# Feed-forward jobs run in pairs, product by product, with in-place quads kept twice

## The chip, the cores and the metric

One NeuronCore of one Trainium2 chip runs the whole kernel. The metric is the device time of one execution in microseconds. The kernel before took 2522.27 us, the median of three runs (2521.65 to 2526.93).

## What is computed

The reference is a trunk of two residual layers on a sequence of 1024 tokens and a width of 1024, all in float32. Layer 0 has a state-space and a gated-recurrence mixer, layer 1 has windowed attention. Behind each mixer comes the part that the change is about:

```
hn = rms_norm(h, mlp_norm[i])                                    # 1024 x 1024
h  = h + square(relu(hn @ w_mlp_in[i])) @ w_mlp_out[i]           # 1024 x 4096, 4096 x 1024
```

An embedding gate follows each of them, and a last RMS norm. The jobs into which it is cut may run in any order that keeps their inputs ahead of them.

## The kernel before, in words

**A float32 product in three passes.** Each operand is split into a high part (rounded to the matmul's type) and a low part (the rest), and each tile product is made of high by high, high by low and low by high. Weights are split while they stream in: ScalarE rounds (`high`, all its instructions stand in the trace at line L1348), VectorE or GpSimd subtracts (`weight_low`, L2323, and `low`, L578).

**Jobs and products.** Both matrix products of the feed-forward block use a 2 by 2 block scheme with seven block products instead of eight. A job is one pair of 128-wide output blocks by both halves of the tokens, with one weight slab of 1 MB, and has seven products, 0 to 6. A product is 12 matmuls of 512 columns (4 contraction tiles by 3 passes), at L1099. There are 32 jobs: 16 up (into the 4096-wide middle), then 16 down in four chunks of four jobs; a chunk uses the middle blocks of four up jobs. So one feed-forward block has 224 products, and the kernel has two such blocks. TensorE takes the jobs one after the other, product by product.

**Weights of a job.** The slab lands in `SRAW` (two buffers in turns, a third for the last job). GpSimd makes four sums of quarters (`sum_`, L573) in `SA` and `SB`, one buffer each, and the low parts of products 0, 3 and 6; VectorE makes the low parts of 1, 2, 4 and 5. High and low parts lie in a ring of five. ScalarE rounds four products ahead, VectorE subtracts three ahead.

**PSUM.** A job has three banks, and two jobs in turns have six. Products 0 and 3 add up in the first, 1, 4 and 6 in the second, 2 and 5 in the third. Between two products of a bank its partial value is read out: product 3 waits for the copy of product 0, product 4 for the eviction of product 1, and so on.

**Behind an up job.** ScalarE copies product 0 to `P1` (`first_product`); VectorE adds bank values to make `U2`, `V5` and the four quads `Q` (`evict_up`, L2332 to L2345), multiplies them by the reciprocal norm (`scaled`, L2350 to L2352), ScalarE does relu and square (`squared`) into four of the seven blocks of `MT`, VectorE makes the other three (`mid_sums`, L2357 to L2362), and SP stores the seven blocks of the job to DRAM in one transfer (L345).

**Refill.** The seven operands `OP` are used by every job of a chunk. When product s of the last job of a chunk is done, SP loads the new block s (L351, 1 MB), ScalarE rounds it in two halves (`cast`), and VectorE subtracts in two halves (`refill`, L2401). Product s of the next job needs it seven products later. There are four refills in a block: ahead of down jobs 16, 20, 24 and 28. In a down job VectorE adds each bank to the residual (`evict_down`, L2374 to L2387).

**Start.** The first job's operands are made from the residual as the projection ahead of it comes out (`x_operands`); operands 4, 5 and 6 are made after that (`x_late`, `cast_late` on ScalarE, `late_difference`, `late_last`, `block_low` on VectorE, L2305 to L2316), and the sums of squares and the reciprocal root follow.

**Order.** Each engine has its order written out by hand: a loop over t, the product that TensorE has reached, with what is due at each t. An engine does its list in order, so a wait holds all that stands behind it.

## Time and profile before

| what | value |
|---|---|
| median of 3 runs | 2522.27 us |
| profiled execution, its own time | 2522.98 us |
| its span, first to last instruction | 2521.2 us |
| TensorE busy | 2321.1 us, 92% |
| VectorE, GpSimd, ScalarE busy | 1611.7, 1066.9 and 980.9 us |
| mean granted TensorE clock | 0.966 of full speed |
| first feed-forward block, its products | 543 to 1218 us of the span |
| second one | 1700 to 2375 us |

The profile is one execution. Busy time is a share of the whole span. A matmul's own duration overlaps the next one's, so the pace is read from how many run in a stretch, and a stretch has to be asked for by its ends. The granted clock is 1.00 at 2.4 GHz and 0.50 at 1.2 GHz; a mean between them mixes both.

### The profile page before, as it was taken

What the parts mean: (1) busy time and instruction counts of PE and PEld (TensorE: products, weight loads), DVE (VectorE), ACT (ScalarE), POOL (GpSimd) and SP (SyncE); (2) the same over time, 40 slices, a digit from 0 to 9 for tenths busy, and PEclk for the clock granted to TensorE, in tenths of its full rate; (3) what the DMA queues carried; (4) which work ended last, traced back from release to release, by engine and by line L of the source; (5) the groups of instructions that cost most, each with busy time, mean ns of one, the idle gap of its engine ahead of it and who ended that gap; (6) DMA issues with size and microseconds to landing.
All of it is one profiled execution on the core that took longest, in us unless ns stands there. A gap on an engine that the chain in (4) does not pass through costs nothing.

```text
span 2521.2 us, 31322 instructions
## 1 busy us (share of the span) xinstructions
PE 2321.1 (92%) x12286; PEld 1858.2 (74%) x12286; DVE 1611.7 (64%) x1959; ACT 980.9 (39%) x1526; POOL 1066.9 (42%) x684
## 2 busy tenths in 40 slices
PE   8998967997999989999998999987999989999997
PEld 6887856776888877777786776665888867877786
DVE  6867279558676766648627355567767676467725
ACT  3120255443444534433312245644444454334315
POOL 4433112234555545545332343634555545455421
PEclk9998978999999999999999999998999999999998
DMA  7372331212344634433113111111444464324111
GB/s 209 106 120 74 112 110 61 92 44 106 138 154 167 224 110 167 167 117 100 51 50 100 40 28 51 59 42 34 168 146 161 153 225 167 118 100 164 54 50 67
DMA packets 216867, 277.85 MB, mean 110 GB/s; under 512 B 32548, under 2 KB 171016, under 8 KB 212616
## 3 DMA queue, kind: packets, MB, share of 16 engines
q1 hardware_dynamic: 203176, 257.13, 30.5%
q10 hardware_dynamic: 13552, 18.81, 3.0%
q8 instruction: 94, 1.54, 0.3%
q14 instruction: 45, 0.37, 0.0%
HBM read 190.53 MB, written 84.21 MB: 109 GB/s over the span
## 4 chain that ended last, share of the span: by engine, by line
PE 71%; DVE 20%; ACT 4%; issue 3%; POOL 1%; ACTq 1%; DMA 0%; DVEq 0%; SPq 0%; POOLq 0%
PE ps L1099 39%; PE ps L727 15%; DVE op L2401 6%; PE ps L1265 3%; PE ps L878 2%; PE ps L1297 2%; DVE st_lo L2323 1%; PE ps L1225 1%; DVE hg_queries_keys L2166 1%; DVE residual L2387 1%; PE ps L1238 1%; PE ps L1249 1%; PE ps L899 1%; PE ps L914 1%; PE ps L794 1%
## 5 line engine op out<-in xcount | busy, mean ns | idle before, releaser
L1099 PE MATMUL ps<-op,st_hi 128*128 128x512 f32 x3584 | 1134.5, 398 | 93.1 <-DVE op L2401 39.3
L1099 PEld LDWEIGHTS ps<-op,st_hi 128*128 128x128 f32 x3584 | 683.1, 192 | 261.8 <-issue 100.3
L1099 PE MATMUL ps<-op,st_lo 128*128 128x512 f32 x1792 | 709.1, 396 | 0.0
L578 POOL TENSOR_TENSOR st_lo<-st_raw,st_hi 128x512 fp32r<-128x512 f32 x192 | 323.9, 1687 | 631.2 <-ACT st_hi L1348 631.2
L1099 PEld LDWEIGHTS ps<-op,st_lo 128*128 128x128 f32 x1792 | 343.5, 192 | 73.3
L1348 ACT ACTIVATE st_hi<-st_sum 128x512 fp32r<-128x512 f32 x256 | 160.3, 630 | 436.6 <-POOL st_sum L573 232.1
L557 POOL CAST w_hi<-w_raw 128x1024 fp32r<-128x1024 f32 x66 | 74.1, 1123 | 482.2 <-issue 249.3
L2387 DVE TENSOR_TENSOR residual<-residual,ps 128x512 f32<-128x512 f32 x192 | 131.3, 684 | 192.6 <-PE ps L1099 191.2
L1348 ACT ACTIVATE st_hi<-st_raw 128x512 fp32r<-128x512 f32 x192 | 120.6, 628 | 262.4 <-PE ps L1099 262.4
L573 POOL TENSOR_TENSOR st_sum<-st_raw 128x512 f32<-128x512 f32 x128 | 180.9, 1413 | 57.9 <-DVE st_lo L2323 57.9
L2323 DVE TENSOR_TENSOR st_lo<-st_sum,st_hi 128x512 fp32r<-128x512 f32 x256 | 193.9, 758 | 0.4
L727 PE MATMUL ps<-x_hi,w_hi 128*128 128x512 f32 x544 | 170.3, 394 | 7.5 <-DVE x_lo L2407 3.7
L727 PE MATMUL ps<-x_lo,w_hi 128*128 128x512 f32 x544 | 167.7, 390 | 0.0
L727 PE MATMUL ps<-x_hi,w_lo 128*128 128x512 f32 x544 | 167.6, 389 | 0.0
L2401 DVE TENSOR_TENSOR op<-op_raw,op 128x1024 fp32r<-128x1024 f32 x112 | 167.1, 1531 | 0.0
L559 POOL TENSOR_TENSOR w_lo<-w_raw,w_hi 128x1024 fp32r<-128x1024 f32 x66 | 161.6, 2448 | 5.3
L1348 ACT ACTIVATE op<-op_raw 128x1024 fp32r<-128x1024 f32 (+2 forms) x150 | 141.1, 988 | 32.3 <-DVE op_raw L2316 21.6
L727 PEld LDWEIGHTS ps<-x_hi,w_hi 128*128 128x128 f32 x544 | 101.0, 188 | 33.4 <-issue 6.6
L727 PEld LDWEIGHTS ps<-x_hi,w_lo 128*128 128x128 f32 x544 | 102.1, 188 | 21.5
L727 PEld LDWEIGHTS ps<-x_lo,w_hi 128*128 128x128 f32 x544 | 102.1, 188 | 21.4
L573 POOL TENSOR_TENSOR st_sum<-st_sum,st_raw 128x512 f32<-128x512 f32 x64 | 98.0, 1531 | 5.0
L573 POOL TENSOR_TENSOR st_sum<-st_raw,st_sum 128x512 f32<-128x512 f32 x64 | 94.3, 1474 | 0.0
(343 smaller groups left out, 3407.4 us busy)
## 6 DMA issues: line engine op xcount, KB each, us to landing
mid_dram<-mid_sums SPq DMA_DIRECT2D x32, 1792.0 KB, 5.7
op_raw<-mid_dram SPq DMA_DIRECT2D x56, 1024.0 KB, 6.1
st_raw<-w_mlp_in_in SPq DMA_DIRECT2D x32, 1024.0 KB, 5.4
st_raw<-w_mlp_out_in SPq DMA_DIRECT2D x32, 1024.0 KB, 5.3
w_raw<-w_in_even_in SPq DMA_DIRECT2D x20, 512.0 KB, 4.5
residual_dram<-residual ACTq DMA_DIRECT2D x2, 4096.0 KB, 12.4
w_raw<-w_ple_gate_in SPq DMA_DIRECT2D x16, 512.0 KB, 4.1
residual<-residual_dram SPq DMA_DIRECT2D x3, 2048.0 KB, 8.6
```

What stands on the lines that cost most here:

```text
L557: pool.tensor_copy(WH[:, b, :], RAW[:, b, :]).then_inc(S["w_hi_done"], 1)
L559: pool.tensor_tensor(WL[:, b, :], RAW[:, b, :], WH[:, b, :].bitcast(F32), ALU.subtract).then_inc(S["w_ready"], 1)
L573: pool.tensor_tensor(o[:, :, :], x, y, op).then_inc(S["st_sum"], 1)
L578: pool.tensor_tensor(SL[r][:, :, :], x, SH[r][:, :, :].bitcast(F32), sub).then_inc(S["st_lo_pool"], 1)
L727: ins = pe.matmul(acc[:, h, :], w[:, k, :], x[:, k0 + k, h * HALF:(h + 1) * HALF], start=(k == 0 and w is wh and x is xh), stop=(k == kts ...
L878: ins = pe.matmul(ACC[u % 2][:, h, :], w[:, k, :], x[:, k, h * HALF:(h + 1) * HALF], start=(k == 0 and w is wh and x is XAh), stop=(k == K ...
L1099: ins = pe.matmul(PS[:, o, :], w[:, j, :], OP[s][:, x, j, :], start=(s < 3 and j == 0 and w is SH[r] and x == 0), stop=(j == 3 and w is SL ...
L1265: ins = pe.matmul(PS[:, h, :], w[:, k, :], x[:, k, h * HALF:(h + 1) * HALF], start=(k == 0 and w is whs[s % 2] and x is XAh), stop=last)
L1348: return act.activation(o, i, f, **kw)
L2323: tt(SL[r][:, :, :], (SB if s in (1, 5) else SA)[:, :, :], SH[r][:, :, :].bitcast(F32), sub).then_inc(S["st_lo"], 1)
L2387: tt(h, h, PS[:, x, :], add).then_inc(S["st_ev"], 1)
L2401: tt(OP[s][:, 1, 2 * h:2 * h + 2, :], OPF[s][:, 1, 2 * h:2 * h + 2, :], OP[s][:, 0, 2 * h:2 * h + 2, :].bitcast(F32), sub)\
```

## The change

The two jobs of a pair are run product by product: 0 of the first, 0 of the second, 1 of the first, and so on, 14 products to a set. Only the last pair keeps the old order. Every engine's list is written for sets. The sum buffers `SA` and `SB`, and the quads `Q`, are there twice. An up job's partial values are built in its own quads (`P1`, `U2` and `V5` are gone); ScalarE copies product 0 and product 3 from PSUM; one VectorE operation takes the maximum with zero and multiplies by the reciprocal norm; ScalarE squares all four quads in place with one instruction; four differences follow, one of them in place, two in `MT` and one in `T4`, which there is once. The stores of a job are three: quads (1 MB), two sums (0.5 MB), last sum (0.25 MB), and the copy of a later job's product 0 waits for the first of these to land. A refill's halves are spread over 14 products, one per product. A first down product is copied by ScalarE. Half of the making of operand 6 goes from VectorE to GpSimd. The blocks' order in DRAM follows the stores.

```diff
+def product_at(n):
+
+    k, r = divmod(n, 2 * SLOTS)
+    b, s = divmod(r, SLOTS) if k == SETS - 1 else (r % 2, r // 2)
+    return 2 * k + b, s
...
+    SA, SB = ([at(f"st_sum{b}{x}", [P, 4, P], F32, MISC_AT + (4 + 4 * b + 2 * x) * K) for b in range(2)] for x in range(2))
+    Q = [at(f"quads{b}", [P, 4, HALF], F32, o) for b, o in enumerate((E1_AT, MISC_AT + 12 * K))]
+    MT = [at(f"mid_sums{b}", [P, 2, HALF], F32, E1_AT + (8 + 4 * b) * K) for b in range(2)]
+    T4 = at("mid_last_sum", [P, HALF], F32, E0_AT + 12 * K)
...
+                def store_set(g):
+                    sp.wait_ge(S["q_ready"], UP * i + g + 1)
+                    sp.dma_start(t_dram[i][g][:, 0:4, :], Q[g % 2][:, :, :]).then_inc(stored[g % 2], 16)
+
+                def store_sums(g):
+                    sp.wait_ge(S["mt_ready"], UP * i + g + 1)
+                    sp.dma_start(t_dram[i][g][:, 4:6, :], MT[g % 2][:, :, :]).then_inc(mt_stored[g % 2], 16)
+
+                def store_last(g):
+                    sp.wait_ge(S["t4_ready"], UP * i + g + 1)
+                    sp.dma_start(t_dram[i][g][:, 6, :], T4[:, :]).then_inc(S["t4_stored"], 16)
...
+                    if k >= SETS // 2 and k % 2 == 0 and r == 0 and k < SETS - 1:
+                        refill((k - SETS // 2) // 2, 6)
+                    if k >= SETS // 2 - 1 and k % 2 and r and r % 2 == 0 and k < SETS - 1:
+                        refill((k - SETS // 2 + 1) // 2, r // 2 - 1)
+                    if 1 <= k <= SETS // 2:
+                        if r == 3:
+                            store_set(g - 2)
+                        if r == 4:
+                            store_set(g - 1)
+                            store_sums(g - 2)
+                            store_last(g - 2)
+                        if r == 5:
+                            store_sums(g - 1)
+                        if r == 6:
+                            store_last(g - 1)
+                    if r in (9, 10) and k < SETS - 1:
+                        b = r - 9
+                        sp.wait_ge(S["st_lo_pool"], low_pool(i, g + b, 6))
+                        raw(g + 2 + b)
+                sp.wait_ge(S["st_lo_pool"], low_pool(i, JOBS - 3, 6))
...
+                    pool.wait_ge(S["st_lo"], low_dve(i, g, 2))
+                    pool.tensor_tensor(sum_of(g, 4), quarter(g, 0, 0), quarter(g, 1, 0), sub).then_inc(S["st_sum"], 1)
+                    pool.tensor_tensor(sum_of(g, 5), quarter(g, 0, 1), sum_of(g, 1), sub).then_inc(S["st_sum"], 1)
...
+                def late_operand():
+                    pool.wait_ge(S["op_x_scaled"], X_SCALED * i + 10)
+                    pool.wait_ge(S["op_x_sum"], X_SUMS * i + 9)
+                    pool.wait_ge(S["op_ready"], READY * i + 12)
+                    pool.tensor_tensor(OPF[6][:, 1, :, :], OPF[6][:, 1, :, :], OP[1][:, 0, :, :].bitcast(F32), sub).then_inc(S["op_x_sum"], 1)
+
+                for k in range(SETS - 1):
+                    for g in (2 * k, 2 * k + 1):
+                        first_sum(g)
+                        low(g, 0)
+                        second_sum(g)
+                    for g in (2 * k, 2 * k + 1):
+                        low(g, 3)
+                    if k == 0:
+                        late_operand()
+                    for g in (2 * k, 2 * k + 1):
+                        last_sums(g)
+                    for g in (2 * k, 2 * k + 1):
+                        low(g, 6)
...
+                for n in range(PRODUCTS):
+                    g, s = product_at(n)
...
+                        x = sum_of(g, s)
                     fn(SH[n % RINGS][:, :, :], x, ACT.Copy).then_inc(S["st_hi"], 1)
 
-                def first_product(g):
-                    act.wait_ge(S["st_prod"], sb + SLOTS * g + 1)
-                    if g:
-                        act.wait_ge(S["st_ev"], ev(i, g - 1, 5))
-                    fn(P1[:, :], PS[:, BANKS[g % 2][0], :], ACT.Copy).then_inc(S["st_p1"], 1)
+                def copy(g, s):
+                    a_, b = BANKS[g % 2][0], g % 2
+                    act.wait_ge(S["st_prod"], made(i, g, s))
+                    if s == 3:
+                        fn(Q[b][:, 0, :], PS[:, a_, :], ACT.Copy).then_inc(S["st_p1"], 1)
+                    elif g < UP:
+                        if g >= 2:
+                            act.wait_ge(*set_stored(i, g - 2))
+                            act.wait_ge(S["t4_ready"], UP * i + g - 1)
+                        elif g == 1:
+                            act.wait_ge(S["ss_done"], norm + 1)
+                        fn(Q[b][:, 1, :], PS[:, a_, :], ACT.Copy).then_inc(S["st_p1"], 1)
+                    else:
+                        act.wait_ge(mt_stored[(g - UP) // 2], 16 * (UP // 2) * (i + 1))
...
-                    act.wait_ge(S["q_scaled"], n + 1)
-                    for h in range(2):
-                        fn(Q[:, 2 * h:2 * h + 2, :], Q[:, 2 * h:2 * h + 2, :], ACT.Relu).then_inc(S["q_relu"], 1)
...
+                cast_late(i, 5, 9, 9)
+                high(9)
...
+                    dve.wait_ge(S["op_x_sum"], X_SUMS * i + 10)
...
+                    _, b_, c_ = BANKS[g % 2]
+                    q = Q[g % 2]
+                    dve.wait_ge(S["st_prod"], made(i, g, s))
+                    if s < 3:
+                        dve.wait_ge(S["st_p1"], copied(i, g, 0))
+                        tt(q[:, 4 - s, :], q[:, 1, :], PS[:, (b_, c_)[s - 1], :], add).then_inc(S["st_ev"], 1)
+                    elif s == 6:
+                        tt(q[:, 1, :], q[:, 1, :], PS[:, b_, :], add).then_inc(S["st_ev"], 1)
                     else:
-                        tt(Q[:, 1, :], P1[:, :], PS[:, b_, :], add).then_inc(S["st_ev"], 1)
+                        dve.wait_ge(S["st_ev"], ev(i, g, 6 - s))
+                        tt(q[:, s - 2, :], q[:, s - 2, :], PS[:, (b_, c_)[s - 4], :], add).then_inc(S["st_ev"], 1)
 
                 def scaled(g):
-                    dve.wait_ge(S["st_ev"], ev(i, g, 5))
+                    q = Q[g % 2]
+                    dve.wait_ge(S["st_ev"], ev(i, g, 6))
+                    dve.wait_ge(S["st_p1"], copied(i, g, 3))
                     dve.wait_ge(S["rstd_done"], norm + 1)
-                    tt(Q[:, 0, :], PS[:, BANKS[g % 2][0], :], RSTD[:, lefts], ALU.mult).then_inc(S["st_c11"], 1)
-                    tt(Q[:, 2:4, :], Q[:, 2:4, :], RSTD[:, rights].unsqueeze(1).to_broadcast([P, 2, HALF]), ALU.mult)
-                    tt(Q[:, 1, :], Q[:, 1, :], RSTD[:, lefts], ALU.mult).then_inc(S["q_scaled"], 1)
-
-                def mid_sums(g):
-                    n = UP * i + g
-                    dve.wait_ge(S["q_squared"], 2 * n + 2)
-                    tt(MT[:, 4, :], MT[:, 5, :], MT[:, 2, :], sub)
-                    tt(MT[:, 2, :], MT[:, 2, :], MT[:, 0, :], sub).then_inc(S["mt_sum"], 1)
-                    dve.wait_ge(S["mt_sum"], 2 * n + 1)
-                    tt(MT[:, 1, :], MT[:, 5, :], MT[:, 2, :], sub).then_inc(S["mt_sum"], 1)
-                    dve.wait_ge(S["mt_sum"], 2 * n + 2)
-                    tt(MT[:, 6, :], MT[:, 3, :], MT[:, 1, :], sub).then_inc(S["mt_ready"], 1)
+                    for h, t in ((0, lefts), (2, rights)):
+                        ins = dve.scalar_tensor_tensor(q[:, h:h + 2, :], q[:, h:h + 2, :], 0.0, RSTD[:, t].unsqueeze(1).to_broadcast([P, 2, HALF]),
+                                                       ALU.max, ALU.mult)
+                    ins.then_inc(S["q_scaled"], 1)
...
+                def first_mid_sums(g):
+                    q, mt, n = Q[g % 2], MT[g % 2], UP // 2 * i + g // 2
+                    dve.wait_ge(S["q_squared"], UP * i + g + 1)
+                    if n:
+                        dve.wait_ge(mt_stored[g % 2], 16 * n)
+                    tt(mt[:, 0, :], q[:, 3, :], q[:, 0, :], sub)
+                    tt(q[:, 3, :], q[:, 2, :], q[:, 3, :], sub).then_inc(S["q_ready"], 1)
+
+                def second_mid_sum(g):
+                    q, mt = Q[g % 2], MT[g % 2]
+                    dve.wait_ge(S["q_ready"], UP * i + g + 1)
+                    tt(mt[:, 1, :], q[:, 2, :], mt[:, 0, :], sub).then_inc(S["mt_ready"], 1)
+
+                def last_mid_sum(g):
+                    dve.wait_ge(S["mt_ready"], UP * i + g + 1)
+                    if i or g:
+                        dve.wait_ge(S["t4_stored"], 16 * (UP * i + g))
+                    tt(T4[:, :], Q[g % 2][:, 1, :], MT[g % 2][:, 1, :], sub).then_inc(S["t4_ready"], 1)
...
-                            return
+                        if c == 1:
+                            dve.wait_ge(S["st_p1"], copied(i, UP + q, 0))
...
+                block_low(4, 17)
+                for s in (1, 2):
+                    evict_up(0, s)
+                weight_low(8)
+                for s in (1, 2):
+                    evict_up(1, s)
+                weight_low(9)
+                block_low(5, 18)
+                weight_low(10)
                 late_last()
+                weight_low(11)
+                evict_up(0, 4)
+                evict_up(1, 4)
                 block_low(6, 19)
...
+                for p in range(2):
+                    reciprocal(p)
+                evict_up(0, 5)
+                evict_up(1, 5)
...
+                    if k < SETS // 2:
+                        if r in (6, 7):
+                            for s in (1, 2):
+                                evict_up(g + r - 6, s)
+                        if r >= 9:
+                            evict_up(g + (r - 9) % 2, 4 + (r - 9) // 2)
+                    if 1 <= k <= SETS // 2 and r == 0:
+                        evict_up(g - 1, 6)
+                    if t > UP * SLOTS and product_at(t - 1) not in COPIES:
+                        evict_down(*product_at(t - 1))
                     if t + 3 < PRODUCTS:
...
+                    if k < SETS // 2 and r == 13:
+                        scaled(g)
+                    if 1 <= k <= SETS // 2:
+                        if r == 0:
+                            scaled(g - 1)
+                        if r == 2:
+                            first_mid_sums(g - 2)
+                        if r == 3:
+                            first_mid_sums(g - 1)
+                            second_mid_sum(g - 2)
+                            last_mid_sum(g - 2)
+                        if r == 4:
+                            second_mid_sum(g - 1)
+                        if r == 5:
+                            last_mid_sum(g - 1)
+                    kj, rj = divmod(t - 6, 2 * SLOTS)
+                    if kj >= SETS // 2 - 1 and kj % 2 and kj < SETS - 1:
+                        refill((kj - SETS // 2 + 1) // 2, rj // 2, rj % 2)
...
+                    if k == SETS - 1 and r < SLOTS and 2 <= r <= 5:
+                        add_squares(after, r - 2)
+                    if k == SETS - 1 and r in (SLOTS + 3, SLOTS + 5):
+                        add_squares(after, 4 + (r - SLOTS - 3) // 2)
```

## Rows read from the trace of the kernel before

**Rows 1.** The page: share of each engine in the chain that ended last.

```profile
PE 71%; DVE 20%; ACT 4%; issue 3%; POOL 1%; ACTq 1%; DMA 0%; DVEq 0%; SPq 0%; POOLq 0%
```

**Rows 2.** Windows, product matmuls alone: stretch, length, busy (count), clock, DMA share, GB/s.

```profile
543.00:624.60 81.60, 60.99 (x240) 0.90 0.18 62
624.60:861.60 237.00, 236.95 (x1045) 1.00 0.42 156
861.60:899.30 37.70, 29.40 (x121) 0.92 0.80 295
899.30:958.80 59.50, 59.50 (x253) 0.96 0.34 122
958.80:988.00 29.20, 23.68 (x97) 1.00 0.57 204
988.00:1044.30 56.30, 56.30 (x241) 0.97 0.29 100
...
1129.80:1161.00 31.20, 25.20 (x97) 0.89 0.54 191
```

**Rows 3.** Timeline of TensorE, 550 to 585 us, where it had been idle.

```profile
557.96 1.19 PE L1099 MATMUL ps<-op,st_hi 128*128 128x512 f32 x2 [5.94 <-ACT p L1348]
...
569.70 0.70 PE L1099 MATMUL ps<-op,st_hi 128*128 128x512 f32 x2 [2.24 <-DVE op L2305]
...
581.21 1.19 PE L1099 MATMUL ps<-op,st_hi 128*128 128x512 f32 x2 [8.51 <-DVE quads L2341]
```

**Rows 4.** Chain, 955 to 990 us: start, us, what.

```profile
960.08 2.27 DVE op L2401 x2
...
964.07 3.36 DVE op L2401 x2
967.43 0.60 DVE residual L2387
```

**Rows 5.** Groups by form, 955 to 990 us: count, busy us, mean ns, idle before.

```profile
L2401 DVE TENSOR_TENSOR op<-op_raw,op 128x1024 fp32r<-128x1024 f32 x14 | 21.8, 1597 | 0.0
...
L578 POOL TENSOR_TENSOR st_lo<-st_raw,st_hi 128x512 fp32r<-128x512 f32 x5 | 8.7, 1743 | 12.2 <-ACT st_hi L1348 12.2
...
L2387 DVE TENSOR_TENSOR residual<-residual,ps 128x512 f32<-128x512 f32 x9 | 6.1, 678 | 4.1 <-PE ps L1099 4.1
...
L573 POOL TENSOR_TENSOR st_sum<-st_raw 128x512 f32<-128x512 f32 x2 | 4.3, 2170 | 3.1 <-DVE st_lo L2323 3.1
```

**Rows 6.** Groups by form, 700 to 738 us, an up stretch.

```profile
L578 POOL TENSOR_TENSOR st_lo<-st_raw,st_hi 128x512 fp32r<-128x512 f32 x6 | 10.4, 1732 | 17.5 <-ACT st_hi L1348 17.5
...
L573 POOL TENSOR_TENSOR st_sum<-st_raw 128x512 f32<-128x512 f32 x4 | 5.2, 1294 | 0.0
...
L1348 ACT ACTIVATE quads<-quads 128x1024 f32<-128x1024 f32 x4 | 4.0, 1042 | 0.0
```

**Rows 7.** Line L2407: count, duration ns min/median/max, first and last start.

```profile
L2407 DVE SCALAR_TENSOR_TENSOR x_lo<-residual,vectors,x_hi x16: 1278/1286/3411, 1213.6 to 2389.3; 128x1024 fp32r<-128x1024 f32 x16
```

**Rows 8.** Timeline of VectorE at the start, operand 6.

```profile
569.48 3.37 DVE L2315 TENSOR_TENSOR op_raw<-op_raw,op 128x2048 f32<-128x2048 f32 x1
```

**Rows 9.** Timeline of GpSimd at the start.

```profile
570.66 3.31 POOL L578 TENSOR_TENSOR st_lo<-st_raw,st_hi 128x512 fp32r<-128x512 f32 x1
```

**Rows 10.** DMA issues: count, KB each, median us to landing.

```profile
mid_dram<-mid_sums SPq DMA_DIRECT2D x32, 1792.0 KB, 5.7
op_raw<-mid_dram SPq DMA_DIRECT2D x56, 1024.0 KB, 6.1
st_raw<-w_mlp_in_in SPq DMA_DIRECT2D x32, 1024.0 KB, 5.4
...
fqig_dram<-stage SPq DMA_DIRECT2D x11, 512.0 KB, 3.1
```

**Rows 11.** Windows, all engines: stretch, length, busy (count), clock, DMA share, GB/s.

```profile
862.00:878.00 16.00, 16.00 (x73) 13.23 (x72) 13.45 (x15) 12.20 (x16) 10.18 (x7) 1.00 1.04 376
988.00:996.00 8.00, 8.00 (x28) 6.45 (x29) 3.51 (x6) 1.27 (x2) 2.91 (x3) 0.79 0.00 0
```

391 lines of the change are left out of this document (185 added, 206 removed).

## The prediction

> **What bounds the kernel now.** The page gives 71% of the last-ending chain to TensorE and 20% to VectorE [rows 1]. That is the mean over very different stretches, so the windows over the product matmuls come next [rows 2]. In a long stretch of up jobs 1045 matmuls take 237.0 us, 0.2268 us each, so a product (12) takes 2.72 us at full clock: the floor. The 2688 matmuls of a block need 609.6 us and take 675.4 us (543.0 to 1218.4). The excess of 66 us is what a new order can win, 132 us in two blocks. Count times 0.2268 taken from each stretch's length puts it in place [rows 2]:
>
> - start (240 matmuls): 81.6 - 54.4 = 27.2 us
> - refill for job 16 (121): 37.7 - 27.4 = 10.3 us
> - refills for 20 and 24 (97 each; the second's row, 1044 to 1073 us, repeats the first's): 29.2 - 22.0 = 7.2 us each
> - refill for 28 (97): 31.2 - 22.0 = 9.2 us
> - stretches right behind refills: 59.5 - 57.4 = 2.1, then 56.3 - 54.7 = 1.6, twice: 5.3 us.
>
> The last item is the clock: in the 8 us behind a refill TensorE is never idle yet runs 28 matmuls instead of 35, at a granted 0.79, a mix of the levels 1.2 and 2.4 GHz, after a stretch with gaps [rows 11].
>
> In a refill the chain is almost all VectorE: two subtractions of 128x1024 take 2.27 us undisturbed and 3.36 us when a GpSimd instruction falls among them; an eviction takes 0.60 [rows 4]. Seven products bring 14 such halves. They have the VectorE full, and product s+7 waits for them.
>
> At the start three gaps stand out [rows 3]: 5.94 us for the copy of product 0 (ScalarE was still making operands), 2.24 us for a late operand, and 8.51 us at product 6, whose operand ends a chain through both engines.
>
> **The change, part by part.** I write r for the product's place in a set of 14; one step is 2.72 us.
>
> *Refills of jobs 20, 24, 28.* Now 14 products (38.1 us) stand between the release of an operand and its need. VectorE owes 14 halves at 1.14 (16.0), 14 evictions at 0.60 (8.4) and 8 low parts at 0.60 (4.8): 29.2 us. GpSimd disturbs: 14 halves in the old refill were busy 21.8 us instead of 16.0 [rows 5], 5.8 us for the 8 or 9 GpSimd instructions beside them, 0.7 each; there will be 14, 9.8 us. Sum 39.0 us against 38.1: level, with seven products' slack for the halves and about two for a low part queued behind one. But in such stretches GpSimd's sums stretch from 1.29 to 2.17 us [rows 5, 6], and a pair's slabs are freed only at r = 9 and 10, so its chain gets tight. Of 7.2 + 7.2 + 9.2 + 3.2 us (the clock items behind them) = 26.8 I leave 5.5: gain 21.3 (bounds 11 and 26.8).
>
> *Refill of job 16.* It meets the end of the last up pair: 10 evictions (6.0), 14 halves (16.0), 8 low parts (4.8), four fused operations, eight differences (4.8), three down evictions (1.8). The fused operation (maximum, then multiply, 128x1024) isn't in the trace; its nearest row is another two-input operation of that class, 1.28 us at the least and 3.41 at the most [rows 7], and a plain one takes 1.14 [rows 4]. I take 1.2, as it stands beside similar work: 4.8. Sum 38.2, with GpSimd 48 us against 38.1: VectorE falls 10 us behind. The deadline it breaks is new: the copy of job 16's product 0 waits until the sums of job 14 are stored, for they share memory, and ScalarE and product 3 wait with it. VectorE's list reaches that sum some 41 us into the window, the store lands about 4 us later, and product 3 is due at 38: a gap of 7 to 8 us. I leave 9.5 of 10.3 + 2.1: gain 3 (bounds -6 and 12.4). DMA is near its limit here too: 376 GB/s at a full share [rows 11].
>
> *Start.* Product 3 comes at place 6, product 4 at 8 and product 6 at 12, so the 5.94 and 2.24 us gaps close, and the chain for operand 6 has 14 us more. Against that, half of operand 6 goes to GpSimd. VectorE's 3.37 us [rows 8] become four times 1.29 = 5.2 us [rows 6], or four times 3.31 = 13 beside a busy VectorE [rows 9]; I take 8, between them, since both engines are half busy there. Four sums and so the weights of product 4 queue behind it: gaps of 2 us at place 8 and 2 us at place 12. Then the reciprocal root is ready only when both jobs are over, `scaled` of both holds VectorE's low parts: 2.5 us. With the first wait for the last operand (3.2), the four norm matmuls (1.5) and a cold clock for a short time (2) I leave 13 of 27.2: gain 14 (bounds 7 and 22). The Trainium skill (GPSIMD Engine Reference, section 3.1) gives 4.5 us for such a float32 operation of 2048 elements, 1.96 times VectorE's. By that the gap at place 8 would vanish and the block be 2 us shorter; the row with both engines busy says the opposite.
>
> *Up jobs.* Now no gap at all [rows 2]. VectorE keeps five evictions and four differences; three multiplications (0.60, 1.14, 0.60) become two of about 1.2; ScalarE drops two relus of 1.04 us [rows 6], gains a copy of about 0.6. All of it lies under TensorE: nothing gained. The new wait is the release of the quads. Second job of a pair: `scaled` done at about 5.7 us of the set, square 7.9, differences 10.7, store sent, landed by 10.7 + 5.4 to 6.1 [rows 10] = 16 to 17, copied 17.5; product 3 of the next job wants it at 19.1. A slack of 1.6 us: I charge 1 us per block (0 to 15). ScalarE waits there with the next `high` behind it, which has two products of slack.
>
> *Nothing elsewhere:* the tail keeps its order, the slabs' size and the matmuls are the same. SP issues 3 stores instead of one and is idle most of the time.
>
> **Sum.** 21.3 + 3 + 14 - 1 = 37.3 us a block; the second block shows the same gaps, so 75 us in two. The profiled execution took 2523.0 us (span 2521.2 plus 1.8), the median 2522.3, so they are alike. Forecast 2522.3 - 75 = 2447 us. Bounds: 26.8 + 12.4 + 22 = 61 a block, 2400 us; 11 - 6 + 7 - 15 = -3, 2528 us, all ends bad at once.
>
> **Rivals.**
> *A. VectorE and GpSimd stay the bound.* If a disturbance costs 1.1 us (3.36 - 2.27) [rows 4] and not 0.7, each set with a refill owes 44.6 us against 38.1, its slack is used up, and the start gains only 7: 11 + 0 + 7 - 1 = 17 a block, 2488 us. For it: the row. Against: not every instruction of GpSimd collided.
> *B. Everything is covered.* 55 us or more a block, 2410 us. Against: job 16's refill.
> *C. The release of the quads is late in every up pair.* The slack of 1.6 us is small. If landing takes 10 us, the store is in at 20.7 and copied at 21.3, 2.2 us late; seven sets in two blocks make 31 us: 2478 us. In its favour, the three stores of a job and those of the next run at once. By the Trainium skill (DMA: Bandwidth & Descriptors, anatomy of one DMA) a transfer from GpSimd costs a fixed 2 us plus its bytes at 436 GB/s: three stores pay the fixed part three times, and 1 MB would land in 4.4 us, before the deadline. The trace agrees, with 5.7 us for 1.75 MB and 3.1 us for 0.5 MB. Those two rows are what speaks against C [rows 10].
> *D. Slower: the slab hand-over.* Both slabs of a pair are used to nearly the end of the set. The first is free at r = 8.9, lands at 10.9 (5.4 us) [rows 10], then GpSimd does sum, low part, sum, sum, low part: 1.29, 1.73, 1.29, 1.29, 1.73 = 7.3 us [rows 6], to r = 13.6. It is due at r = 15, a slack of 3.9 us. It decides from the point where landing plus those five take over 3.9 us more. At 2.17 us for each sum it's 2.6 more, inside. Only if landing took 10 us as well would each of 30 hand-overs lose 3.3 us, 99 us in all: 2447 + 99 = 2546 us.
> *E. No difference:* the gaps move and keep their size; 2522.
>
> **Chances.** Forecast 0.60, A 0.16, B 0.12, C 0.07, D 0.04, E 0.01. The range leaves out D and about half of B and takes in A and C: 2412 to 2490. A measurement of this kernel can tell about 0.2% (5 us) from no change. Faster 0.95, same 0.01, slower 0.04.
>
> **What would show it.** The stretch from the first product to job 2's end should take 14 us less; gaps before 20, 24 and 28 nearly gone, VectorE still about 95% busy there; one gap of 7 to 8 us in job 16 at product 3, released by a ScalarE copy that waited for a store; the clock at 1.00 behind refills; the up sets without gaps. Wrong would be: gaps in each up set before product 3 of the second job (C), gaps before products 0 and 1 of each pair (D), or GpSimd's busy time up by over a tenth (A).

## The result, and the profile after

The changed kernel takes 2493.76 us, the median of four runs (2487.47 to 2495.61). The kernel before took 2521.96 us beside it (2521.4 to 2526.93). The ratio is 0.988, its 95% interval 0.9861 to 0.9898: faster, by 28 us, which is 1.2% and clear of the scatter. The forecast was 2447 us and 75 us faster, in a range of 2412 to 2490. So the sign was right and the size was wrong: 28 of 75 us came, and the time lies above the range.

The profiled execution took 2494.89 us (span 2493.2). Its page, busy time of four engines and the chain's shares:

```profile
PE 2314.5 (93%) x12286; PEld 1860.1 (75%) x12286; DVE 1642.3 (66%) x1917; ACT 939.2 (38%) x1470; POOL 1092.2 (44%) x686
...
PE 64%; DVE 18%; issue 5%; ACT 5%; DMA 4%; POOL 2%; ACTq 1%; SPq 0%; DVEq 0%; POOLq 0%
```

DMA was 0% of the chain [rows 1] and is 4% now, half of it for slabs of the down weights; VectorE went from 20% to 18%. The shares don't say which wait is new; the windows and the timelines do. The windows over the product matmuls (now at line L1202) of the first block show where, with the columns of [rows 2]:

```profile
543.00:640.00 97.00, 83.55 (x333) 0.91 0.24 82
640.00:820.00 180.00, 177.04 (x776) 1.00 0.41 149
820.00:860.10 40.10, 35.03 (x155) 0.97 0.60 209
860.10:923.00 62.90, 53.40 (x214) 0.91 0.53 189
923.00:985.00 62.00, 62.00 (x275) 1.00 0.50 166
985.00:1132.00 147.00, 147.00 (x650) 1.00 0.47 158
1132.00:1204.50 72.50, 66.89 (x286) 0.98 0.15 44
```

With the floor of 0.2268 us a matmul the excess of each part is its length less its count times 0.2268:

| part of the block | before | forecast | after | how the last is worked out |
|---|---|---|---|---|
| start | 27.2 | 13 | 21.5 | 97.0 - 333 x 0.2268 |
| up jobs | 0 | 1 | 4.0 | 180.0 - 776 x 0.2268 |
| refill for job 16, with the end of the last up pair | 12.4 | 9.5 | 19.3 | 103.0 - 369 x 0.2268 |
| refills for 20, 24 and 28 | 26.8 | 5.5 | 6.8 | 281.5 - 1211 x 0.2268 |

The four add up to 51.6 us where 66.4 were before, 14.8 us a block. Measured from the first product matmul to the last, the first block went from 677.6 to 662.1 us and the second from 683.6 to 667.4, 31.7 us in all. Between the blocks 2.9 us were lost, the start and the tail of the span changed by under 1 us: 28.0 us of the span.

So the largest term held within 1.3 us, and three did not hold. A place is a product's position in the block, counted from 0; a set of a pair has 14 places. These are the stalls of TensorE in the first block (timeline, what it waited for in brackets; smaller ones of 0.2 to 1.3 us are left out):

```profile
569.18 1.19 PE L1202 MATMUL ps<-op,st_hi 128*128 128x512 f32 x2 [4.22 <-ACT quads L1451]
601.90 1.22 PE L1202 MATMUL ps<-op,st_hi 128*128 128x512 f32 x2 [2.72 <-DVE st_lo L2447]
616.31 1.19 PE L1202 MATMUL ps<-op,st_hi 128*128 128x512 f32 x2 [4.57 <-ACT quads L1451]
...
860.15 1.19 PE L1202 MATMUL ps<-op,st_hi 128*128 128x512 f32 x2 [5.13 <-ACT quads L1451]
...
907.78 1.19 PE L1202 MATMUL ps<-op,st_hi 128*128 128x512 f32 x2 [7.58 <-issue]
1135.22 0.73 PE L1202 MATMUL ps<-op,st_hi 128*128 128x512 f32 x2 [2.14 <-DVE st_lo L2447]
1141.00 1.22 PE L1202 MATMUL ps<-op,st_hi 128*128 128x512 f32 x2 [2.76 <-DVE st_lo L2447]
```

**The refills of 20, 24 and 28.** No stall stands ahead of jobs 20 and 24, and the clock is 1.00 behind them, where the stretch of before had 0.79 [rows 11]. A half still takes 1616 ns on the mean, much as in [rows 5], but now 38.1 us lie between release and need. By form, VectorE from 923 to 985 us, around the refill for 20:

```profile
L2518 DVE TENSOR_TENSOR op<-op_raw,op 128x1024 fp32r<-128x1024 f32 x12 | 19.4, 1616 | 4.2 <-ACT op L1451 4.2
L2510 DVE TENSOR_TENSOR residual<-residual,ps 128x512 f32<-128x512 f32 x18 | 12.3, 683 | 16.4 <-PE ps L1202 16.4
L2447 DVE TENSOR_TENSOR st_lo<-st_sum,st_hi 128x512 fp32r<-128x512 f32 x12 | 11.0, 923 | 1.5 <-ACT st_hi L1451 1.5
```

VectorE was nearly never free in the refill of before (4.1 us, [rows 5]); here it is idle 22 us of 62. This window holds 12 of the 14 halves and nine products ahead of them; while the halves run, VectorE is busy 32.0 us of 38:

```profile
947.00:985.00 38.00, 32.00 (x33) 1.00 0.58 195
```

That is 84%, where the forecast had about 95%. The stalls of 2.14 and 2.76 us in the refill for 28 come where the last chunk adds the stored first sums to the residual.

**The first stall of the start, 4.22 us.** Product 3 of job 1 needs the copy of job 1's product 0. On ScalarE that copy stands behind the rounding for product 8, which waits for a sum of GpSimd. Three timelines, ScalarE's, GpSimd's and VectorE's:

```profile
567.92 0.63 ACT L1451 ACTIVATE st_hi<-st_sum 128x512 fp32r<-128x512 f32 x1 [7.02 <-POOL st_sum L664]
568.46 0.58 ACT L1451 ACTIVATE quads<-ps 128x512 f32<-128x512 f32 x1
```

```profile
559.95 4.61 POOL L676 TENSOR_TENSOR op_raw<-op_raw,op 128x2048 f32<-128x2048 f32 x1
564.51 3.32 POOL L664 TENSOR_TENSOR st_sum<-st_raw 128x512 f32<-128x512 f32 x1
```

```profile
561.00 5.70 DVE L2430 TENSOR_TENSOR op<-op_raw,op 128x2048 fp32r<-128x2048 f32 x1 [3.57 <-ACT op L1451]
```

The operand's half that the change gave to GpSimd took 4.61 us, where I had taken 8. That agrees with the Trainium skill (GPSIMD Engine Reference, section 3.1: 4.5 us). The sum behind it took 3.32 us, as [rows 9], and VectorE's operation beside both took 5.70 us, where one of that size had taken 3.37 [rows 8]. The three rows read as waits for each other's end: VectorE's started at 561.0, GpSimd's ended at 564.5, and VectorE's ended 2.1 us behind that, about what it takes alone (2.28 at 572.5); the sum started at 564.5 and ended 1.1 us behind VectorE's, about as long as an undisturbed one (1.29). The stall is at place 7 and about as long as the two of 2 us that I had for places 8 and 12; GpSimd's late operand delays it, as I had it, but through the copy and not through the weights of product 4.

**The other two stalls of the start.** They stand in the chain behind the root. ScalarE's timeline, ahead of it:

```profile
595.14 0.63 ACT L1451 ACTIVATE st_hi<-st_sum 128x512 fp32r<-128x512 f32 x1 [3.57 <-POOL st_sum L660]
595.79 1.28 ACT L1451 ACT_TABLE_LOAD   x1
597.09 1.06 ACT L1451 ACTIVATE rstd<-rstd 128x1024 f32<-128x1024 f32 x1
```

VectorE, which had ended its reciprocals at 592.5, stood 4.39 us until the root, then did two fused operations, and the low part for product 17 behind them came late (2.72 us). Squares, differences and last sum follow, and the copy of job 2's product 0 waits for the last sum (4.57 us). The expectations below speak of this stall as the one in front of job 2's first product; what waits is product 3, whose bank that copy empties. The 2.72 us stand at place 17; where an expectation says product 15, this one is meant.

**The refill of job 16.** The gap at its product 3 is 7.58 us, as forecast (7 to 8 us). TensorE's row names no releaser (`issue`), so ScalarE's timeline has to say what the copy stood for: first a sum of GpSimd, then the store.

```profile
903.03 0.63 ACT L1451 ACTIVATE st_hi<-st_sum 128x512 fp32r<-128x512 f32 x1 [5.88 <-POOL st_sum L664]
907.09 0.60 ACT L1451 ACTIVATE p_sum<-ps 128x512 f32<-128x512 f32 x1 [3.42 <-DMA mid_dram<-mid_sums]
```

The other one, 5.13 us ahead of product 3 of job 15, was not in my sum. VectorE waits with job 13's last sum until job 12's has been stored, since there is one buffer of them, and the copy of job 15's product 0 waits for it (VectorE, then ScalarE):

```profile
858.60 0.69 DVE L2489 TENSOR_TENSOR mid_last_sum<-quads,mid_sums 128x512 f32<-128x512 f32 x1 [4.65 <-DMA mid_dram<-mid_last_sum]
```

```profile
859.41 0.60 ACT L1451 ACTIVATE quads<-ps 128x512 f32<-128x512 f32 x1 [5.51 <-DVE mid_last_sum L2489]
```

The tile's own view says how such a store lands, and who waits for the sums in the whole run:

```profile
  ACT quads L1451: 62.3, 28
...
DMA to landing us min/median/max: 2.0/2.4/7.9
```

The late one is a transfer of 256 KB, issued at 850.58 us in the middle of three refill loads of 1 MB (841.5, 846.9, 852.6) and four other stores of 0.5 and 1 MB. In the up sets the same sum is the last thing that the copy waits for, 28 times: that is where the stalls of 0.2 to 1.3 us come from.

The medians from issue to landing, against [rows 10]:

```profile
op_raw<-mid_dram SPq DMA_DIRECT2D x56, 1024.0 KB, 5.2
...
mid_dram<-quads SPq DMA_DIRECT2D x32, 1024.0 KB, 3.9
...
mid_dram<-mid_sums SPq DMA_DIRECT2D x32, 512.0 KB, 3.5
```

### The profile page after: what moved, and what is told of

Read it like the earlier page. It is cut to its first block, busy times and chain, and to the rows that moved or that the text cites. A ratio compares the mean times of both kernels' runs of the same rounds, so it can differ in the third digit from the quotient of the medians.

```text
span 2493.2 us, 31423 instructions
## 1 busy us (share of the span) xinstructions
PE 2314.5 (93%) x12286; PEld 1860.1 (75%) x12286; DVE 1642.3 (66%) x1917; ACT 939.2 (38%) x1470; POOL 1092.2 (44%) x686
## 4 chain that ended last, share of the span: by engine, by line
PE 64%; DVE 18%; issue 5%; ACT 5%; DMA 4%; POOL 2%; ACTq 1%; SPq 0%; DVEq 0%; POOLq 0%
PE ps L1202 32%; PE ps L831 15%; PE ps L1368 3%; PE ps L982 2%; DMA st_raw<-w_mlp_out_in 2%; PE ps L1400 2%; DVE st_lo L2447 2%; DVE mid_sums L2483 2%; DVE mid_last_sum L2489 1%; ACT quads L1451 1%; PE ps L1328 1%; POOL st_lo L670 1%; DVE quads L2478 1%; DVE stage L1953 1%; DVE hg_queries_keys L2291 1%
## 5 line engine op out<-in xcount | busy, mean ns | idle before, releaser
L1202 PE MATMUL ps<-op,st_hi 128*128 128x512 f32 x3584 | 1128.7, 397 | 74.3 <-ACT quads L1451 31.7
L1202 PEld LDWEIGHTS ps<-op,st_hi 128*128 128x128 f32 x3584 | 682.5, 191 | 233.4 <-issue 61.7
L1202 PE MATMUL ps<-op,st_lo 128*128 128x512 f32 x1792 | 706.7, 394 | 0.0
L670 POOL TENSOR_TENSOR st_lo<-st_raw,st_hi 128x512 fp32r<-128x512 f32 x192 | 306.0, 1596 | 525.6 <-ACT st_hi L1451 524.8
L1202 PEld LDWEIGHTS ps<-op,st_lo 128*128 128x128 f32 x1792 | 342.2, 191 | 73.1
L2447 DVE TENSOR_TENSOR st_lo<-st_sum,st_hi 128x512 fp32r<-128x512 f32 x256 | 230.7, 910 | 10.9 <-ACT st_hi L1451 9.5
L2518 DVE TENSOR_TENSOR op<-op_raw,op 128x1024 fp32r<-128x1024 f32 x112 | 175.6, 1568 | 39.4 <-ACT op L1451 39.4
L1451 ACT ACTIVATE op<-op_raw 128x1024 fp32r<-128x1024 f32 (+2 forms) x150 | 147.0, 990 | 8.3 <-DVE op_raw L2439 5.8
L654 POOL TENSOR_TENSOR st_sum<-st_raw 128x512 f32<-128x512 f32 x64 | 86.6, 1352 | 107.2 <-DMA st_raw<-w_mlp_out_in 64.4
L831 PEld LDWEIGHTS ps<-x_hi,w_lo 128*128 128x128 f32 x544 | 102.1, 188 | 21.5
L2460 DVE TENSOR_TENSOR quads<-quads,ps 128x512 f32<-128x512 f32 x64 | 43.7, 685 | 112.4 <-PE ps L1202 112.4
L664 POOL TENSOR_TENSOR st_sum<-st_raw 128x512 f32<-128x512 f32 x64 | 113.2, 1768 | 6.5 <-DVE st_lo L2447 6.5
```

The source lines that it names most:

```text
L654: pool.tensor_tensor(sum_of(g, 2), quarter(g, 1, 0), quarter(g, 1, 1), add).then_inc(S["st_sum"], 1)
L664: pool.tensor_tensor(sum_of(g, 4), quarter(g, 0, 0), quarter(g, 1, 0), sub).then_inc(S["st_sum"], 1)
L670: pool.tensor_tensor(SL[r][:, :, :], x, SH[r][:, :, :].bitcast(F32), sub).then_inc(S["st_lo_pool"], 1)
L831: ins = pe.matmul(acc[:, h, :], w[:, k, :], x[:, k0 + k, h * HALF:(h + 1) * HALF], start=(k == 0 and w is wh and x is xh), stop=(k == kts ...
L1202: ins = pe.matmul(PS[:, o, :], w[:, j, :], OP[s][:, x, j, :], start=(s < 3 and j == 0 and w is SH[r] and x == 0), stop=(j == 3 and w is SL ...
L1451: return act.activation(o, i, f, **kw)
```

## The experiments

Each is the changed kernel with the edit shown or named; runs 12 to 14 start from the kernel of run 11. The first eight are one run each, beside the kernel before on the same chip (2527.87 us for the first four, 2527.17 for the next four). Since single runs scatter by some microseconds, I also give the length of the two feed-forward blocks in the profile, first product matmul to last. All are collected at the end of this section. They scatter too. In the six kernels that leave the start as it is (changed, 1, 2, 5, 6, 7), product 3 of job 2 comes 72.5 to 74.4 us after the first product in the first block and 78.6 to 80.5 in the second. In the six that change nothing between there and product 3 of job 16 (changed, 3, 4, 7, 8, 9), this stretch takes 288.2 to 291.5 us. So a block that differs by under some 4 us in one profile shows little by itself.

**1. The first down products of jobs 16 and 17 stay in PSUM (z_psum).** They no longer wait for the memory of the stored sums, and are moved there later, at r = 11 and 12.

```
 copy(g, s), g = 16, 17:
-    act.wait_ge(mt_stored[...]); act.wait_ge(S["t4_ready"], ...)
-    fn(Z1[g - UP][:, :], PS[:, a_, :], ACT.Copy)
+    fn(PS[:, 4 + g - UP, :], PS[:, a_, :], ACT.Copy)
```

> The changed kernel, but the first products of jobs 16 and 17 are copied at once into two PSUM banks that are free by then, and moved to SBUF five products later, so that job 16 waits for no store. Theory S (the 7.6 us gap of job 16 before its product 3 is the store of job 14's sums, which shares memory with the copy): that gap goes in both blocks, and what is left is below 3 us, about 2 x 8 us and some clock less, 2476 to 2480 us in all. Rival V (VectorE is simply too far behind there and the store wait only hides it): another gap of 5 us or more takes its place at product 3, 4 or 5 of job 16, released by VectorE, and the time stays within 5 us of 2494.

2487.66 us, ratio 0.984; blocks 2.1 and 4.9 us shorter. The stall at product 3 of job 16 fell from 7.58 to 4.06 us (in the second block from 7.60 to 4.09) and not to nothing: the wait for the store was 3.5 us of it. That lies between my two cases. What is left comes from GpSimd's timeline in this run, and ScalarE's:

```profile
891.73 8.28 POOL L670 TENSOR_TENSOR st_lo<-st_raw,st_hi 128x512 fp32r<-128x512 f32 x2 [7.78 <-ACT st_hi L1451]
```

and, with the window ended at 894 us, the first of the two alone:

```profile
891.73 6.61 POOL L670 TENSOR_TENSOR st_lo<-st_raw,st_hi 128x512 fp32r<-128x512 f32 x1 [7.78 <-ACT st_hi L1451]
```

```profile
901.77 0.63 ACT L1451 ACTIVATE st_hi<-st_sum 128x512 fp32r<-128x512 f32 x1 [5.89 <-POOL st_sum L664]
902.31 0.58 ACT L1451 ACTIVATE ps<-ps 128x512 f32<-128x512 f32 x1
```

One low part took 6.61 us and the next about 1.7, where the median of the run is 1.30 and the mean 1.6. VectorE ran from 891.3 to 897.1 without a break, each instruction with two inputs in SBUF and not slowed (0.68 and 1.21 us). The late low part ended 1.2 us after VectorE's first instruction with an input in PSUM had started (897.11). So it looks shut out and not slow; the rows show it, no run tests it. The copy stands in the queue behind a rounding that waits for the sum behind those low parts. The low part's excess of 5.3 us is more than the 4.06 us that are left.

**2. The refill for job 16 four products later (shift4).** Loads, roundings and subtractions are all moved by four places.

```
-                    kj, rj = divmod(t - 6, 2 * SLOTS)
+                    kj, rj = divmod(t - 6 - (4 if t < 14 * (SETS // 2 + 1) else 0), 2 * SLOTS)
```

> The changed kernel, with the refill for job 16 (loads, roundings, subtractions) four products later than now; the other refills stay. Theory D (the refill's loads and the seven stores of the last up pairs want the DMA at once, and the single buffer of the last sum, 7.9 us to landing there against a median of 2.4, holds VectorE and then ScalarE's copy): the 5.1 us gap before product 3 of job 15 goes, the last sum of job 12 lands in under 4 us, 2 x 5 us less. Rival V (VectorE's total work of 48 us in 38 is the cause): the same lateness comes four products later, the excess of this refill stays at 17 to 20 us a block and the time within 5 us of 2494.

2476.35 us, ratio 0.980; blocks 10.3 and 6.9 us shorter. The stall of 5.13 us is gone (0.27 left); the one at product 3 of job 16 grew from 7.58 to 9.27. The crowd of transfers was the cause of the first one: with the loads moved out of it, the store of the last sum lands in time (issued at 845.35, the next last sum runs at 848.65 without a wait). The roundings and subtractions moved too, but VectorE had stood 4.65 us for that store, so it was not short of time there. The gain of 17 us is more than the 10 I expected; some of it is scatter, since the two blocks differ by 3.4 us.

**3. On ScalarE the copy goes ahead of the rounding of product 8 (copy_first).**

```
-                high(8)
                 copy(1, 0)
+                high(8)
```

> The changed kernel, with one line of ScalarE's list moved: the copy of job 1's product 0 ahead of the rounding for product 8. Theory Q (the 4.2 us gap before product 7 is this copy standing behind a rounding that waits for GpSimd's sums, which wait for operand 6): the gap before product 7 is gone; the next one is product 8 for its low part, 1 to 2 us, so 2 to 3 us less a block, 2488 to 2490. Rival P (the start is bound by GpSimd's chain for operand 6 anyway): the gap moves to product 8 in full, 4 us, and the time is unchanged.

2494.11 us, ratio 0.987; blocks 0.2 and 1.5 us shorter, which is nothing. The stall of 4.22 us became 1.95, but two of GpSimd (0.61 and 2.47) came in before product 17. It was moved, not removed; the block is as long as before within the scatter.

**4. The late operand's half back on VectorE (operand6_vector).**

```
-                    if k == 0:
-                        late_operand()
 late_last():
+                    tt(OPF[6][:, 1, :, :], OPF[6][:, 1, :, :], OP[1][:, 0, :, :].bitcast(F32), sub)
```

> The changed kernel, with the first half of operand 6 put back on VectorE. Theory P (GpSimd's 4.6 us operation, with 5.7 us for the VectorE operation beside it, is what delays the start): the gap before product 7 shrinks from 4.2 to about 0 and nothing replaces it, up to 4 us less a block. Rival: VectorE has no room at the start either, its list gets 3.4 us longer, and a gap of 3 us or more appears at product 10 or 12, so the time is unchanged or higher.

2489.01 us, ratio 0.985; blocks 0.4 and 5.2 us shorter. The first stall became 0.37, and in its place stand 1.72, 2.45 and 1.15 us for low parts of GpSimd, then 2.31 and 4.43 as before. Product 3 of job 2 comes at 72.0 us and not at 72.5: again the start is not shorter in the first block.

**5. One and two together (shift4_z).**

> Both edits at job 16's refill: four products later, and the first products of jobs 16 and 17 copied into free PSUM banks. With the later refill alone the gap before product 3 of job 16 was 9.3 us, with the PSUM copies alone 4.1. Theory W (the copy has two waits in a row: the store, and behind it the rounding that stands ahead of it on ScalarE and waits for GpSimd's sums, which are held up by VectorE's unbroken run): with both edits the gap is 3 to 6 us and released by GpSimd's sums, 4 us less a block than the later refill alone, 2467 to 2470. Rival (the store alone was what counted, and the 4.1 us came from the crowd that the later refill has thinned out): gap under 1.5 us, 2460 or less.

2467.65 us, ratio 0.976; blocks 12.5 and 12.6 us shorter. The two gains add up in the blocks: 12.4 for the first, 11.8 for the second. The gap at product 3 of job 16 is 4.06 us and the rounding ahead of the copy waited 5.89 us for a sum of GpSimd, as the first case said. The rival, that the 4.06 us came from the crowd of transfers, is out: the crowd is gone and they stay.

**6. The same with six products (shift6_z).**

> As the run before with the refill six products later instead of four, one product short of its last possible place. Theory W: VectorE's refill halves then fall almost wholly into job 16 and 17's own products, where its other work is light after the first six products; two more products of distance give a gap 1 to 2 us smaller at product 3. Rival: the slack of the halves is used up, product 0 or 1 of job 18's chunk mates is not touched but products 3 to 6 of job 16 wait for their operands; gaps released by L2518's kind of instruction appear and the time is 3 us or more above that of the run before.

2481.75 us; blocks 5.3 and 6.6 us longer than with four. Stalls of 1.57, 3.38 and 5.44 us stand there, released by the subtractions of the refill (`op`). So the halves do have slack, but not the seven products that I had put: it ends between four and six. The rival held.

**7. The stored first sums added three products later in the last chunk (z_late).**

> The changed kernel, with the two additions of the saved first product to the residual moved from product 0 to product 3 of jobs 28 to 31, that is behind the last refill. Theory Z (the 2.1 and 2.8 us gaps at jobs 28 and 29 are these additions, 1.8 us each with a wait of VectorE for itself of 1.1 to 1.5 us ahead, on a VectorE that is full with refill halves): both gaps shrink to under 1 us, 4 us and some clock less a block, 2484 to 2487. Rival R (the refill is late there because its slab landed after 9.3 us): gaps stay.

2492.41 us; blocks 1.7 us longer and 4.8 shorter. The stalls of 2.14 and 2.76 us before job 28 were replaced by these, of the same run's TensorE:

```profile
1146.10 0.73 PE L1202 MATMUL ps<-op,st_hi 128*128 128x512 f32 x2 [0.23 <-DVE st_lo L2447]
1150.26 0.73 PE L1202 MATMUL ps<-op,st_hi 128*128 128x512 f32 x2 [1.14 <-DVE st_lo L2447]
```

and by others of 3.11, 1.76 and 1.13 us later. In the first block 2.6 us of other stalls, at places 14 and 15, came in as well; they are not the edit's, run 1 has them too. From product 3 of job 16 to the end the blocks are 2.8 us longer and 1.5 shorter. So moving the additions gained nothing: they cost VectorE the same wherever they stand.

**8. The low part of product 17 ahead of the fused operations (low_first).**

```
-                    if t + 3 < PRODUCTS:
+                    if t + 3 < PRODUCTS and t != 14:
                         weight_low(t + 3)
+                    if t == 13:
+                        weight_low(17)
```

> The changed kernel, with the low part for product 17 made ahead of the fused operations of job 0, which wait for the reciprocal root. Theory L (the 2.7 us gap at product 17 is this low part queued behind the root): that gap is gone in both blocks. Whether time is gained: if the next gap, 4.6 us before product 3 of job 2, is set by the chain root, fused operations, squares, differences, last sum, copy, then it grows by what was won, 7.3 us, and the time is unchanged; if it is set by the order of VectorE's list, 2 to 3 us less a block.

2486.65 us, ratio 0.984; blocks 3.1 and 1.7 us shorter. The stall of 2.72 us is now 2.27 and waits for an eviction; that of 4.57 is 4.38. Up to product 3 of job 2 that is 0.5 and 0.7 us, no gain. In all eight runs the root had come 52.8 to 55.2 us after the first product. That pointed at the root itself.

**9. The root ahead of the rounding (root_first), four executions.**

```
-                    if t + 4 < PRODUCTS:
-                        high(t + 4)
                     if t == 2 * SLOTS - 1:
                         act.wait_ge(S["rcp_done"], norm + 1)
                         fn(RSTD[:, :], RSTD[:, :], ACT.Sqrt)
+                    if t + 4 < PRODUCTS:
+                        high(t + 4)
```

> ScalarE takes the root of the statistics ahead of the rounding of product 17 instead of behind it. In the changed kernel that rounding waited 3.57 us for GpSimd's second sum (whose raw slab had landed late), the reciprocals had been ready since 592.5, and the root came at 597.1. My theory now: the first four sets' stalls hang on the chain reciprocals, root, fused scaling, squares, differences, last sum, copy, and the rounding in front of the root lengthens it by about 3.5 us. Then the root comes 49 to 50 us after the first product instead of 53.3, the stall in front of product 15 (2.72 us) falls under 1 us, that in front of job 2's first product (4.57 us) to 1 to 2 us, and the time drops by 4 to 6 us a block, 8 to 12 in all. Rival (the late raw slabs and GpSimd's sums behind them bound the start, whatever stands in front of the root): the weight of product 17 and the next ones come later by what the root takes (2.3 us with its table load), a stall of POOL or of a low part appears between products 16 and 20, and the time stays within 3 us of the changed kernel.

2482.86 us, the ratio to before 0.9834 (0.9818 to 0.985) against the changed kernel's 0.988; blocks 6.1 and 4.4 us shorter. ScalarE's timeline:

```profile
588.43 1.28 ACT L1451 ACT_TABLE_LOAD   x1
589.73 1.06 ACT L1451 ACTIVATE rstd<-rstd 128x1024 f32<-128x1024 f32 x1
```

The first product stood at 540.6 here, so the root comes 49.1 us behind it and not 53.3. The stall of 2.72 us is 0.53. That ahead of job 2's product 3 stayed at 4.71, but it ends 69.2 us after the first product and not 72.5. In the second block it ends at 77.1 us and not at 80.5. So the root's own gain is 3.3 us a block against the changed kernel, and at least 3.3 and 1.5 against all that leave the start alone. The rest of the 6.1 and 4.4 lies where the edit does nothing: the up sets' small stalls are 1.8 us shorter in the first block and the same in the second. The total is what I expected, the way to it was not: I had looked for it in both stalls.

**10. The joint operation undone alone (relu_scalar), four executions.** VectorE multiplies, ScalarE does relu in place before its square.

```
-                            dve.scalar_tensor_tensor(q[...], q[...], 0.0, RSTD[...], ALU.max, ALU.mult)
+                            tt(q[...], q[...], RSTD[...], ALU.mult)
 squared(g):
+                    fn(Q[g % 2][:, :, :], Q[g % 2][:, :, :], ACT.Relu)
```

> The joint operation is undone alone: VectorE multiplies by the root only (two tensor_tensor of 128x1024) and ScalarE does relu over the quad (128x2048) before its square, still in place and in pairs. It puts about 1.9 us of ScalarE a job into the way from the up product to the last sum, on which the copy of the next job of the same parity waits with no slack (stalls of 0.2 to 1.25 us already stand there). Theory (that way is at its limit in the up sets): about 1.9 us more for each of the seven later up sets' first product at least, and perhaps twice that where both jobs of a pair are hit: 13 to 27 us a block, 25 to 55 us in all. Rival (ScalarE has room in a pair, with 1 to 2 us of slack hidden by the order): stalls in the up sets stay under 1 us each and the time rises by under 10 us. VectorE's operation alone: tensor_tensor of 128x1024 takes 1.1 to 1.3 us as the joint one does (1.28), so it gives back nothing.

2505.14 us, ratio 0.9913 (0.9893 to 0.9934); blocks 6.9 and 5.3 us longer. In each up set two stalls stand now, of 0.7 to 1.4 us, as here in the fourth set:

```profile
693.56 0.70 PE L1202 MATMUL ps<-op,st_hi 128*128 128x512 f32 x2 [0.90 <-ACT quads L1451]
```

Between my two cases: the way from the up product to the last sum is at its limit (each set has longer stalls), but 1.9 us more on it cost about 0.8 for each of the eight sets, 11 us and not the 25 or more that I had. By the medians the joint operation is worth 11 us of the change's 28, by the ratios 8.

**11. Three things together (best), five executions.** Refill four products later, first down products in PSUM, root ahead of the rounding.

> The changed kernel with three things put together: the refill for job 16 four products later, the first products of jobs 16 and 17 kept in PSUM until the stored sums are out, and the root ahead of the rounding. Run one by one they took 2493.8 down to about 2476 (four products later), 2468 (with the PSUM copy) and by my theory 8 to 12 less for the root. If the gains add up: 2457 to 2463. If the start's stalls only move (the rival of the root's run): 2466 to 2472. Against the kernel before (2522) either is a ratio of 0.974 to 0.981.

2463.02 us (2460.62 to 2465.01), ratio 0.9756 (0.9743 to 0.977). It beats both kernels, the changed one by 31 us, and stands at the edge of my first case (2457 to 2463). Blocks 15.8 and 14.7 us shorter than in the changed kernel, where the parts by themselves had 12.5 + 6.1 and 12.6 + 4.4. That fits a root worth 3.3 and 1.5 us up to product 3 of job 2 (69.2 and 77.1 us, against 72.5 and 78.6 in run 5), with the rest of run 9's blocks being scatter. What stays in the first block:

```profile
565.53 1.19 PE L1201 MATMUL ps<-op,st_hi 128*128 128x512 f32 x2 [4.19 <-ACT quads L1450]
...
609.34 1.19 PE L1201 MATMUL ps<-op,st_hi 128*128 128x512 f32 x2 [4.71 <-ACT quads L1450]
...
887.74 1.19 PE L1201 MATMUL ps<-op,st_hi 128*128 128x512 f32 x2 [4.06 <-issue]
...
1121.69 1.22 PE L1201 MATMUL ps<-op,st_hi 128*128 128x512 f32 x2 [2.71 <-DVE st_lo L2456]
```

**12. The same, with job 0's sums ahead of job 1's differences (best_sums), eleven executions.**

```
                         if r == 3:
-                            first_mid_sums(g - 1)
                             second_mid_sum(g - 2)
                             last_mid_sum(g - 2)
+                            first_mid_sums(g - 1)
```

> The three things put together (2463.0 us), and one more: of a pair's middle sums the first job's second and last sum go ahead of the second job's first differences. In every run so far TensorE stood 4.4 to 4.7 us in front of the first product of job 2: its copy had waited for job 0's last sum, and on VectorE the two differences of job 1 (1.77 us each beside GpSimd's sums) stood in front of it. My theory (that chain is the stall's cause and nothing else is as late): the last sum comes 3.5 us earlier, the stall falls from 4.7 to about 1.2 us in each block, the stalls of 0.2 to 0.5 us in the other up sets go for the first job of each pair, and the time is 5 to 9 us lower: 2454 to 2458. Rival (the second job's last sum or the next low parts take its place: its squares and sums come just as much later): a stall of 1 to 4 us appears in front of job 3's first product or of job 2's second, and the time stays within 3 us of 2463.

2519.47 us (2508.05 to 2524.14), ratio 0.9972: 56 us were lost by moving two subtractions of a pair. From the third set on every up set has a stall of 2.6 to 3.1 us, but for one of 1.40; a set takes 42.6 us and not 38.6, as the clock falls too (0.91 to 0.96 in windows of 40 us, where `best` has 1.00). VectorE's timeline in the third set, where it makes the second pair's sums, and SyncE's DMA queue beside it:

```profile
649.99 1.66 DVE L2498 TENSOR_TENSOR mid_last_sum<-quads,mid_sums 128x512 f32<-128x512 f32 x1
...
661.39 0.69 DVE L2498 TENSOR_TENSOR mid_last_sum<-quads,mid_sums 128x512 f32<-128x512 f32 x1 [2.95 <-DMA mid_dram<-mid_last_sum]
```

```profile
648.27 7.14 SPq L394 DMA_DIRECT2D mid_dram<-quads  x2
...
655.93 0.92 SPq L402 DMA_DIRECT2D mid_dram<-mid_last_sum  x1
```

and the same queue without the edit (best):

```profile
640.65 3.74 SPq L394 DMA_DIRECT2D mid_dram<-quads  x2
...
647.45 0.32 SPq L402 DMA_DIRECT2D mid_dram<-mid_last_sum  x1
```

The last sum ended at 651.6, but its store was issued at 655.9. SyncE's list has the quads of the pair's second job ahead of it, and these are ready only behind the moved differences. Without the edit the sum ended at 647.3 and went out at 647.45.

**13. With SyncE's order moved as well (best_sums_sp), four executions.**

```
                         if r == 4:
-                            store_set(g - 1)
                             store_sums(g - 2)
                             store_last(g - 2)
+                            store_set(g - 1)
```

> The kernel with job 0's second and last sums ahead of job 1's first differences took 2519.5, 56 us more than without that, with stalls of 2.6 to 3.1 us in front of every up set's first product. In its trace SyncE's queue sends the quads of a pair's second job ahead of the last sum of its first: with the differences moved back the quads' store was issued late, the last sum's store stood behind it (655.9, where the sum was ready at 651.6), and VectorE waited 2.95 us for that store with the one buffer of last sums. Here SyncE's order is moved as well: sums and last sum of the first job ahead of the second job's quads. My theory (the queue's order alone made the loss, and the moved sums do what I expected of them): the stalls in the up sets fall under 0.6 us, that in front of job 2's first product to 1 to 3 us, and the time comes to 2455 to 2463. Rival (the second job's sums are now late by themselves: two more differences stand in front of its last sum, and the wait for the store stays): stalls of 1 us and more stay in front of every up set's first or second product, and the time is 2468 to 2510.

2468.77 us (2464.9 to 2471.89), ratio 0.9766: 51 of the 56 us are back, so the queue's order made the loss. The stalls of the up sets are 0.15 to 0.84 us again. But nothing is gained over 2463.0. The stall ahead of product 3 of job 2 is split, not shortened:

```profile
611.56 0.71 PE L1201 MATMUL ps<-op,st_hi 128*128 128x512 f32 x2 [1.82 <-ACT quads L1450]
618.36 1.19 PE L1201 MATMUL ps<-op,st_hi 128*128 128x512 f32 x2 [3.81 <-ACT quads L1450]
```

Job 3's copy is late in place of job 2's. On that point the rival of run 12 was right.

**14. Three things together, and the copy ahead of the rounding of product 8 (best_copy), four executions.**

> The three things put together (2463.0), and ScalarE takes the copy of job 1's first product ahead of the rounding of product 8, as in the run where that alone was done. There it gained nothing (2494.1): the stall of 4.2 us in front of job 1's fourth product fell to 2, and other stalls came. My reading was that the root then bounded the start. With the root ahead of its rounding that bound is 6 us earlier. If it is gone: the start's stalls fall by 2 us a block or more and the time to 2457 to 2461. Rival (late raw slabs and low parts of GpSimd bound the products behind it anyway): what is gained at product 7 comes back as POOL or DVE stalls at products 11 to 14, and the time stays at 2461 to 2466.

2465.56 us (2461.54 to 2467.5), ratio 0.9754: no difference to best. The stall of 4.19 us became 1.98, and GpSimd's low parts are waited for 1.71 and 2.47 us. The rival held: with the root earlier (by 4.2 us in run 9, not by 6), the start still gives nothing back for this edit.

The blocks, first product matmul to last, in us:

| kernel | first | second |
|---|---|---|
| before | 677.6 | 683.6 |
| changed | 662.1 | 667.4 |
| z_psum | 660.0 | 662.5 |
| shift4 | 651.8 | 660.5 |
| copy_first | 661.9 | 665.9 |
| operand6_vector | 661.7 | 662.2 |
| shift4_z | 649.6 | 654.8 |
| shift6_z | 654.9 | 661.4 |
| z_late | 663.8 | 662.6 |
| low_first | 659.0 | 665.7 |
| root_first | 656.0 | 663.0 |
| relu_scalar | 669.0 | 672.7 |
| best | 646.3 | 652.7 |
| best_sums | 673.0 | 680.7 |
| best_sums_sp | 651.3 | 654.2 |
| best_copy | 648.7 | 654.4 |

## Why the prediction was wrong

**Refills of 20, 24 and 28: right.** Forecast 5.5 us left of 26.8, measured 6.8. The work of VectorE fits between release and need, and the clock stays up; the windows show it. What happens when the slack is used up is seen at job 16 in run 6. That the sum agrees within 1.3 us is partly luck. I had the work level with the time and something left at each refill; VectorE is busy 84% there, and nothing is left at 20 and 24. The rest stands all at and behind job 28, at the additions of the stored sums, which my list of VectorE's work for that refill left out.

**Refill of job 16: the step that failed.** I had written "VectorE's list reaches that sum some 41 us into the window, the store lands about 4 us later" and took one gap of 7 to 8 us. That gap is there, 7.58 us. But I asked of that window only what job 16 waits for, and not what the last up pair, which runs in the same window, waits for. It waits for a store of 256 KB that takes 7.9 us among the refill's loads instead of 2.4. The stalls of this part sum to 14.6 us (5.13, 0.88, 0.98 and 7.58) and the lower clock around them (0.86 behind the last) makes up most of the other 4.7 us: 19.3 us, where 9.5 were forecast. A "gain 3" became a loss of 6.9, beyond its lower bound of -6. I had the warning in hand (376 GB/s at a full share, [rows 11]) and set no price on it. Run 2 takes this stall away and gets 17 us over both blocks. And of the 7.58 us only 3.5 were the store (run 1); for the other 4 the copy stands on ScalarE behind a rounding, and that behind a GpSimd low part that took 6.6 us. My sum has no term for that queue. No run removes it, so this part is read from the rows.

**Start: the step that failed second.** 21.5 us are left where I forecast 13; the gain of 5.7 is below its lower bound of 7. The pieces, forecast and measured: 2 us at place 8 against 4.22 at place 7; 2 us at place 12 against nothing; 2.5 us behind the root against 2.72; 6.7 us for the first wait, the norm's matmuls and the clock against 10.0; and a stall of 4.57 us at job 2 that was not in the sum, since I followed the root's chain to `scaled` and not on to square, differences, last sum and the copy that waits for it. A part of what bounded it was not seen by me either: the root stands on ScalarE behind a rounding which waits for a sum of GpSimd. Runs 3, 4 and 8 took one stall each down and got it back elsewhere; run 9, which moved the root, is the one that gained, 3.3 us a block up to product 3 of job 2.

**Up jobs: mis-sized.** Forecast 1 us a block, measured 4.0. I had reckoned the release of the quads by the stores' landing, 1.6 us of slack for the second job. The quads' store was never what the copy waited for last; the last sum was, 28 times (62.3 us of ScalarE's time, most of it not on the path). And a last sum takes 1.16 us on the median beside GpSimd, where my list had 0.60. The joint operation cost what I took: 1.21 us a piece in one up set's window, 1.28 over the up sets, against 1.2.

**The rivals.** C named the right wait in the right place (the copy of an up pair's second job: all but one of the small stalls stand at its product 3, the sign I had given for C), but by the wrong store and at four times the price (31 us against 8). A, the two vector engines as the bound, gave 2488 us, nearest to the result, and still is not what happened: it left 15.8 us in the refills of 20, 24 and 28, where 6.8 are, and job 16 as it was, where 6.9 us were lost. Its sign, GpSimd's busy time up by over a tenth, did not come: 1066.9 to 1092.2 us, 2.4%. D cost nothing at the hand-overs of the up sets. Only in the start is a low part of GpSimd waited for, 0.6 to 2.5 us. Such stalls come and go with the order in runs 3, 4 and 14, but also without an edit there: 1.5 and 1.1 us at places 14 and 15 stand in the first block of runs 1, 7 and 13 and not in the changed kernel's, whose second block has them. Whether they, or the count of instructions between root and first sums, set the floor of the start isn't settled. A second buffer for the last sum would test the window of job 16 more cleanly than run 2; no run has it.

**Sum.** Forecast 21.3 + 3 + 14 - 1 = 37.3 us a block. Measured 20.0 - 6.9 + 5.7 - 4.0 = 14.8. The two failed steps are 9.9 and 8.3 us a block, the mis-sized ones 3.0 and 1.3.

## What to carry to other kernels

When work is moved into a window, list every wait that ends in that window, those of the work that was there before too, and price each transfer by its landing beside the others and not by its median. A store that frees the only copy of a small buffer is as critical as the engine that fills it. Where engines and the DMA queue each have a list, move a step in all of them: two subtractions moved on VectorE alone cost 56 us, with the stores moved along 6, little more than the scatter. A stall that reappears a few products later each time it is removed is a sign to look further up. Here the root was a part of the cause and not all of it: run 14, with the root early, still only moved the first stall. And where a merged row of a timeline gives one time for two instructions, look at them one by one before taking the mean: here it hid one of 6.6 us and one of 1.7.

## What the runs showed of the hardware

- **GpSimd beside an unbroken VectorE.** A subtraction of 128x512 took 1.30 us on the median and 6.61 us at most, there beside seven VectorE instructions in a row, each with two inputs in SBUF and none slowed:

```profile
L670 POOL TENSOR_TENSOR st_lo<-st_raw,st_hi x192: 1263/1298/6608, 526.7 to 2330.3; 128x512 fp32r<-128x512 f32 x192
```

  The 3.31 us of [rows 9], which I had taken as the upper bound, is not the most that can happen. The 4.61 us of the late operand, which started while VectorE was idle, agree with the figure cited above.
- **And the other way.** VectorE's 128x2048 subtraction took 5.70 us beside GpSimd's, 2.28 and 3.04 a little later in the same start; its 128x512 sums 1.78 against 0.68. In the start the excess is the time to the end of the other engine's instruction. Which of the two engines goes first isn't settled by these rows: at 891.7 us GpSimd got no turn for 5 us, at 845 to 852 us in the changed kernel the two took turns, each some 1.7 us (VectorE 1.78, GpSimd 1.74).
- **A small transfer in a crowd.** 256 KB took 2.4 us from issue to landing on the median, and 7.9 us among 1 MB loads.
